# A two-block float32 network on one core: joint high and low products in the feed-forwards, squares added on GpSimd, and a first input in halves

## The reference, cut to what matters

```
x = x + 0.5 * swiglu(rms_norm(x, g), w_gate, w_up, w_down)      # four times, 1024 -> 2816 -> 1024
swiglu(h) = (silu(h @ w_gate) * (h @ w_up)) @ w_down
```

## Time and profile before

| | before |
|---|---|
| median of three runs | 2832.76 us |
| the profiled execution | 2852.74 us, its span 2851.3 us |
| TensorE busy | 2691.2 us (94%) |
| VectorE busy | 2021.0 us (71%) |
| ScalarE busy | 1560.1 us (55%) |
| GpSimd busy | 181.0 us (6%) |
| mean granted TensorE clock | 0.964 |

### The profile page before, as it was taken

How to read it: one execution, slowest core, us unless ns; L and a number is a source line. 1 busy time by engine, 2 the same in 40 slices (tenths; PEclk the granted TensorE clock), 3 DMA queues, 4 the chain that set the end, 5 groups by cost and what they waited for, 6 DMA issues and landing times.

```text
span 2851.3 us, 46825 instructions
## 1 busy us (share of the span) xinstructions
PE 2691.2 (94%) x19546; PEld 2453.9 (86%) x19546; DVE 2021.0 (71%) x2781; ACT 1560.1 (55%) x2162; POOL 181.0 (6%) x207
## 2 busy tenths in 40 slices
PE   7998899999898899999899996999999999999998
PEld 7997799999887888998899996788888888888887
DVE  5656755665565455658655675988989898988996
ACT  4445454444431224443544534786777777776785
POOL 1000000000002216001320010000000000000000
PEclk9999999999999769999999998999999999999999
DMA  6442234444333004453345431988989898988993
GB/s 231 178 178 104 104 134 178 179 177 178 138 121 117 3 3 178 179 187 134 122 178 179 157 134 65 376 342 313 355 336 354 332 355 342 355 334 313 357 371 119
DMA packets 84326, 605.09 MB, mean 212 GB/s; under 512 B 9368, under 2 KB 9496, under 8 KB 11472
## 3 DMA queue, kind: packets, MB, share of 16 engines
q1 hardware_dynamic: 81872, 594.05, 55.2%
q10 hardware_dynamic: 1888, 4.85, 0.5%
q0 software_dynamic: 352, 3.15, 0.3%
HBM read 600.96 MB, written 1.05 MB: 211 GB/s over the span
## 4 chain that ended last, share of the span: by engine, by line
PE 84%; DVE 11%; ACT 3%; issue 1%; DMA 1%; ACTq 0%; DVEq 0%
PE bank L396 82%; DVE weights_lo L386 2%; DVE arena L1884 2%; PE bank L2346 1%; ACT weights_hi L378 1%; DVE source_lo_scratch L1319 0%; DVE rstd L447 0%; DVE arena L503 0%; DMA raw_weights<-in_ffn_w_gate 0%; PE bank L807 0%; DMA x_T<-in_x 0%; DVE arena L1907 0%; PE bank L1488 0%; DVE arena L986 0%; DVE normed_T L454 0%
## 5 line engine op out<-in xcount | busy, mean ns | idle before, releaser
L386 DVE TENSOR_TENSOR weights_lo<-raw_weights,weights_hi 128x1024 fp32r<-128x1024 f32 x820 | 996.4, 1231 | 431.1 <-ACT weights_hi L378 424.7
L378 ACT CAST weights_hi<-raw_weights 128x1024 fp32r<-128x1024 f32 x820 | 853.1, 1050 | 472.1 <-PE bank L396 431.0
L396 PE MATMUL bank<-source_hi,weights_hi 128*128 128x256 f32 x2400 | 692.7, 289 | 56.6 <-DVE weights_lo L386 23.7
L396 PE MATMUL bank<-source_lo,weights_hi 128*128 128x256 f32 x2400 | 686.6, 286 | 0.0
L396 PE MATMUL bank<-source_hi,weights_lo 128*128 128x256 f32 x2400 | 686.3, 286 | 0.0
L396 PEld LDWEIGHTS bank<-source_hi,weights_hi 128*128 128x128 f32 x2400 | 468.4, 195 | 61.6 <-issue 36.4
L396 PEld LDWEIGHTS bank<-source_lo,weights_hi 128*128 128x128 f32 x2400 | 468.5, 195 | 1.0 <-issue 0.7
L396 PEld LDWEIGHTS bank<-source_hi,weights_lo 128*128 128x128 f32 x2400 | 468.2, 195 | 0.0
L396 PE MATMUL bank<-weights_hi,source_hi 128*128 128x512 f32 (+1 forms) x960 | 380.3, 396 | 0.0
L396 PE MATMUL bank<-weights_lo,source_hi 128*128 128x512 f32 (+1 forms) x960 | 368.6, 384 | 0.0
L396 PE MATMUL bank<-weights_hi,source_lo 128*128 128x512 f32 (+1 forms) x960 | 367.6, 383 | 0.0
(11 more groups left out here) (350 smaller groups left out, 3353.3 us busy)
## 6 DMA issues: line engine op xcount, KB each, us to landing
raw_weights<-in_exp_in SPq DMA_DIRECT2D x134, 1024.0 KB, 4.9
arena<-in_exp_in SPq DMA_DIRECT2D x90, 1024.0 KB, 4.9
raw_weights<-in_exp_w SPq DMA_DIRECT2D x67, 1024.0 KB, 5.0
arena<-in_exp_w SPq DMA_DIRECT2D x45, 1024.0 KB, 5.1
raw_weights<-in_ffn_w_gate SPq DMA_DIRECT2D x44, 1024.0 KB, 4.8
raw_weights<-in_ffn_w_up SPq DMA_DIRECT2D x44, 1024.0 KB, 4.9
raw_weights<-in_ffn_w_down SPq DMA_DIRECT2D x44, 1024.0 KB, 4.8
raw_weights<-in_dense_w SPq DMA_DIRECT2D x33, 1024.0 KB, 4.8
```

Source lines behind the costliest of these rows:

```text
L378: k.act.copy(k.weights(j)[0], raw_half(k, j)).then_inc(k.w_hi_ready, 1)
L386: k.dve.tensor_tensor(lo, raw_half(k, j), hi.bitcast(F32), ALU.subtract).then_inc(k.w_ready, 1)
L396: return k.pe.matmul(dst, lhsT, rhs, start=start, stop=stop, skip_group_check=shared)
```

## The change

1. In the five feed-forwards, gate and up take a joint product: the two source parts lie in one tile, and the high weights are multiplied with both in one matmul of 512 columns. Its high half goes to columns 0 to 255 of a bank and its low half to columns 256 to 511. The low weights by the high source are added into the first 256. So gate and up of a hidden block need one bank each: banks 0 to 3 for unit 0 and 4 to 7 for all later units. ScalarE copies the low half out of the bank, VectorE adds the high half to it (`low`, `total`), and only then come the root and the silu. The silu of the gate now stands ahead of the last weight split of up. Waits move with it: a later unit's gate waits for the sum of the gate before, and up for that of the up before; the first down also waits until unit 0's banks are empty.
2. The squares of a half feed-forward are added on GpSimd in three steps (4, 2 and 1 blocks), and TensorE takes one matmul against ones.
3. At the start x comes in two halves with a semaphore each, the constants are asked for without a wait, the first weight unit comes in two halves, and the first weight half is split after two source blocks, the second and third behind all of them, ahead of the squares. A tiny copy on ScalarE comes before any input is there.
4. `source_from_norm_vector` scales the blocks itself and makes the low part of block i-2 behind the scaling of block i.

The core of the diff:

```diff
+def mm_both(k, bank, w, at, kt):
+    here = slice(kt * T, (kt + 1) * T)
+    mm(k, bank[:, :].rearrange("p (w t) -> p w t", w=2), w[0][:, at], k.source_both[:, :, here], kt == 0, False, True)
+    return mm(k, bank[:, 0:T], w[1][:, at], k.source[0][:, here], False, kt == KT - 1, True)
+
+def unit_banks(k, i):
+    return [[k.bank[(4 if i else 0) + 2 * b + part] for part in range(2)] for b in range(2)]
...
-            squares_tensor(k, f, 7, KT)
+            k.pe.wait_ge(*k.square_sum.at((f, 1)))
+            mm(k, k.bank[7][:, 0:T], k.con("ones"), blk(k.sq, 0), True, True).then_inc(*k.norm_sums.step((f, "square")))
...
# ffn_scalar, per unit
+        split_both(split_hi, k, gate_name, first + i)
+        split_hi(k, up_name, first + i, 0)
+        k.act.wait_ge(*k.taken(gate_name, first + i))
+        for b in range(2):
+            low(i, b, k.act_buf, 0)
+        if not first_late:
+            silus(i)
+        split_hi(k, up_name, first + i, 1)
+        for b in range(2):
+            k.act.wait_ge(*(tr.products.at((f, i)) if b == 0 else k.taken(up_name, first + i)))
+            low(i, b, k.xn, 1)
+        if first_late:
+            root_scalar(k, f, 7, D, "eps_rms")
+            silus(i)
...
# ffn_vector, per unit
+        split_both(split_lo, k, gate_name, first + i)
+        split_lo(k, up_name, first + i, 0)
+        for b in range(2):
+            total(i, b, k.act_buf, 0, "gate_sum")
+        if late and i > 0:
+            for b in range(2):
+                rooted(i, b, k.act_buf, "gate_sum", "gate")
+        split_lo(k, up_name, first + i, 1)
+        for b in range(2):
+            total(i, b, k.xn, 1, "bank")
...
# half_ffn_scalar for the first feed-forward
+        elif i == 0:
+            k.act.wait_ge(k.params_landed, 16)
+            k.act.wait_ge(k.x_landed[0], 16)
+        elif i == 2:
+            split_hi(k, "ffn_w_gate", 0, 0, 1)
+        elif i == KT // 2:
+            k.act.wait_ge(k.x_landed[1], 16)
...
+    if which == 0:
+        for most in (2, 3):
+            split_hi(k, "ffn_w_gate", 0, 0, most)
...
+def half_ffn_gpsimd(k, which):
+    f = f"half{which}"
+    n = KT // 2
+    k.pool.wait_ge(*k.norm_roots.at((f, "square", KT - 1)))
+    while n > 0:
+        k.pool.tensor_tensor(k.sq[:, 0:n * T], k.sq[:, 0:n * T], k.sq[:, n * T:2 * n * T], ALU.add)\
+            .then_inc(*k.square_sum.step((f, n)))
+        k.pool.wait_ge(*k.square_sum.at((f, n)))
+        n //= 2
...
# source_from_norm_vector
+    for i in range(KT + 2):
+        if i < KT:
+            k.dve.scalar_tensor_tensor(blk(z, i), blk(z, i), k.col(gain, layer * KT + i), k.rstd[:, :], ALU.mult,
+                                       ALU.mult).then_inc(*k.normed.step((f, "scaled", i)))
+        if i >= 2:
+            k.dve.wait_ge(*k.src_hi.at((fill, i - 2)))
+            k.dve.scalar_tensor_tensor(low(i - 2), blk(z, i - 2), k.col(bias, layer * KT + i - 2), ...
```

More of the change, by code:

```diff
@@ L356, in raw_half, with ahead @@
     return k.raw_slots[k.slot[n]][:, part * HALF:(part + 1) * HALF]
-def ahead(k, name, i, part, done):
+def ahead(k, name, i, part, done, most=HALVES):
     n = k.unit[name, i]
@@ L369, in ahead, with split_hi @@
         done += 1
-def split_hi(k, name, i, part=None):
-    for j in ahead(k, name, i, part, k.hi_done):
-        if k.halves[j][1] == 0:
+def split_hi(k, name, i, part=None, most=HALVES):
+    for j in ahead(k, name, i, part, k.hi_done, most):
+        if j == 0:
+            k.act.wait_ge(k.first_landed, 16)
+        elif j == 1 or k.halves[j][1] == 0:
             k.act.wait_ge(*k.landed(k.halves[j][0]))
@@ L379, in split_hi, with split_lo @@
         k.hi_done = j + 1
-def split_lo(k, name, i, part=None):
-    for j in ahead(k, name, i, part, k.lo_done):
+def split_lo(k, name, i, part=None, most=HALVES):
+    for j in ahead(k, name, i, part, k.lo_done, most):
         hi, lo = k.weights(j)
@@ L576, in down_tensor @@
         k.pe.wait_ge(*tr.hidden.at((f, i, b, "lo")))
+        if i == 0 and b == 0:
+            k.pe.wait_ge(*tr.hidden.at((f, 0, 1, "bank")))
         for c in range(KT):
@@ L596, in ffn_scalar @@
             piece = blk(k.act_buf, j)
-            if late:
-                k.act.wait_ge(*tr.hidden.at((f, i, b, "gate")))
-                k.act.activation(piece, piece, ACT.Silu).then_inc(*tr.gates.step((f, i, b, "silu")))
-            else:
-                k.act.wait_ge(*(tr.products.at((f, i)) if b == 0 else k.taken(up_name, first + i)))
-                if i >= 2:
-                    k.act.wait_ge(*tr.hidden.at((f, i - 2, b, "lo")))
-                k.act.activation(piece, k.bank[4 + j][:, 0:T], ACT.Silu).then_inc(*tr.gates.step((f, i, b, "silu")))
@@ L605, in ffn_scalar @@
-            k.act.wait_ge(*tr.hidden.at((f, i, b, product)))
-            if i >= 2:
-                k.act.wait_ge(*k.taken(down_name, first + i - 2))
-            k.act.copy(blk(k.hidden[0], j), piece).then_inc(*tr.gates.step((f, i, b, "hi")))
-        if i > 0:
-            split_both(split_hi, k, down_name, first + i - 1)
-    split_both(split_hi, k, down_name, first + n - 1)
-def ffn_vector(k, f, tr, names, first, n, late=False, scale=None):
-    gate_name, up_name, down_name = names
-    for i in range(n):
-        for name in (gate_name, up_name):
-            split_both(split_lo, k, name, first + i)
-        if late and i == 0:
-            root_vector(k, f)
+            k.dve.wait_ge(*tr.gates.at((f, i, b, "silu")))
```

144 lines of the change are left out of this document (86 added, 58 removed).

## The result

| | before | after |
|---|---|---|
| median of 20 runs each, us | 2833.16 (2830.63 to 2852.03) | 2809.78 (2799.03 to 2836.09) |
| profiled execution, us | 2852.74 | 2827.23 (span 2825.8) |

The ratio after to before is 0.9915, with a 95% interval of 0.9895 to 0.9934: 23.4 us faster between the medians (the interval reaches from 19 to 30 us). Between the two profiled executions it is 25.5 us. I had forecast 2790 from a sum of 42.8.

The account below looks back on a forecast made before the run. TensorE was taken as the bound, with 84% of the span. Terms 23.3 + 12.0 + 7.7 - 1.5 + 2.3 - 1.0 = 42.8 us, subtracted from the median of 2832.8, gave 2790 us; range 2776 to 2812.

Parts of the forecast that it names:

- rival A: Gate and up products: the wide product saves next to nothing, 19 to 23.3 us lost, time 2810; chance 0.12.
- Triples: Gate and up blocks: one 512- and one 256-column product take 0.346 us against 0.360; 1710 x 13.6 ns = 23.3 us gained.
- Squares: Four half feed-forwards: seven products against ones fewer in each, 28 x 0.43 = 12.0 us gained if GpSimd's sums are in time.
- Start: Kernel start: first product at 11.3 us instead of 18.86; gain 7.7 us (5 to 9.5).
- GpSimd's lock: Attention tables' additions on GpSimd hold VectorE: TensorE's wait grows from 4.0 to about 5.5 us, taken as -1.5.
- Steady units: Later feed-forward units: added copies and additions on ScalarE and VectorE stay hidden with 2.4 us of slack; costed at nothing.
- the ring: ScalarE's order: up copies wait for TensorE's last up product, the next weight casts stand behind them and the silus; slack 2.4 us.
- rival C: Steady units: ScalarE's strict order exceeds the slack and each of 51 units pays; at 4 us over, 2872 us; chance 0.04.
- The unit-0 term: First unit of four half feed-forwards: TensorE may wait up to 1 us for a weight half; 0.25 each, 1.0 lost.
- Norms: Low parts made between scalings let TensorE start after 1.85 us instead of 3.80 at the dense norm; 2.3 us gained over three norms.

Follow-up runs that it names:

- the repeat: The changed kernel run again with no edit: median 2824.43 us of 10 runs, ratio 0.9951 to the kernel before.
- the bench: A small kernel without the network: trains of 24 pairs from ready memory, each behind something else; 0.3535 us a pair, 0.3465 right behind a float32 product.

## Why the prediction was right, and where its sum was not

Faster was right, and the time is inside the range, near its slow end, where rival A stood. That it lies inside owes something to luck: ten more runs of the same kernel had a median of 2824.43, outside the range. Their median clock was 0.964 against 0.9705, and the prediction had no term for the clock. The sum of 42.8 is 17 too high against the 25.5 between the two profiles, in which the recurrent stage happened to be equal (306.4 and 306.5). Two fifths of the forecast gain did not come.

- **Triples.** "1710 x 13.6 ns = 23.3 us" is the term that failed most. Measured 6.7 ns a triple by the trace, 6.1 by taking the joint product out and 6.6 by the dense stage with the old norm on both sides (4.3 there with the new norm): about 11 us in all. I had added the paces of two trains of one width each; mixed, they mostly cost 7 ns more. Rival A's result came about (half the gain gone, 12 us instead of its 20) by a mechanism that it named only as "no such mix of widths in this trace": its two pieces cost nothing. The Trainium skill's 2.5 ns for the fixed part of a product (TensorE: Matmul & The Clock Gate, the section on the back-to-back issue gap) is not borne out either: trains of 256 and 512 columns still show 13 ns each.
- **Squares.** 12.0 us counted; TensorE's train is 3.0 us shorter, as said. About 9 are left in the stages; in the first one the sums hold VectorE. They were in time everywhere.
- **Start.** 7.7 counted, 6.9 by the traces (TensorE is past the squares at 36.42 before and at 26.54 after, and 3.0 of the 9.9 are the squares), 7.9 in the repeat (25.56), 5.8 to 6.7 by undoing it. The step that was off: a first half of x at 8.0; it landed at 9.17. The term had the parameters as the only bound from below and left out the constants, which are now asked for at once; whether they held x up was not tried.
- **GpSimd's lock.** -1.5 counted, -1.25 in the profile (4.03 to 5.28); in the versions that leave it as it is the waits were 4.2 (the repeat, 0.86 and 3.38), 4.7, 4.9 and 4.9. Right, on the dear side.
- **Steady units.** Costed at nothing, and no wait for weights stands in them outside GpSimd's additions: the ring of rival C has slack. The unit-0 term, 0.25 in each of four, is there: in the second feed-forward the product at 391.09 comes 0.58 us behind that of the pair before instead of 0.35, and in the first one the wait is 0.55 to 0.82 in four profiles. The second feed-forward still gained 5.3, as 24 of its pairs ran at the fast pace.
- **Norms.** +2.3 counted. At the dense one the wait fell by 1.98 (my "1.9"), of which about 1.2 stayed. At the two second norms "the next split waits behind it and is needed 11 us on" was wrong: it was needed at 1581.8, when its remainder ended at 1583.8. That cost 3.1 and 1.7 us. The term is near -3.6.

The corrected terms: 11.5 + 9 to 12 + 6.3 - 1.25 - 3.6 = 22 to 25. Against them stand 25.5 between the profiles, of which about 1.6 is the clock in the third feed-forward.

The subtraction from the runs' median was unsafe. I took the 20 us between before's profile and its median for noise to be kept apart. They lie on the line of time against clock (0.964 and 0.973), and in the changed kernel's two profiles such a difference is that of the recurrent stage; its runs have their own share of it.

A version that keeps the joint product, the sums and the start, and writes x late, is the better one: ratio 0.9865 (0.9829 to 0.9900) against the kernel before, and 4.3 us under the changed kernel at equal clock, though by four runs only. Holding back the tables' additions gives 3 more at equal clock (2796.2), though its median of 9 runs, five of them at a clock of 0.967 or less, does not show it.

## What to carry to other kernels

Take the pace of a mixed train from a mixed train: two paces measured apart did not add up here (0.3535 against 0.347). When an engine's queue is put in another order, find what stands behind the moved work at each of its uses, not at the one you looked at: the same edit won 1.2 us at one norm and lost 4.8 at two. Where runs spread by more than the effect, plot time against granted clock first, and compare stages cut at common waits.

## What the runs showed of the hardware

- A 512-column and a 256-column product in turn take 0.3535 us or 0.347. In the bench the fast pace stood only right behind a float32 product and was gone with one 256-column product between; in the network whole units had it without one (0.3471 from 591.12 on). Grouped by four a pair takes 0.351. What chooses the pace is open.
- An operand read as two pieces costs what one piece costs (0.3535 both; 0.227 both for trains of it).
- The recurrent stage, 64-wide products, took 282.5 to 311.8 us in profiles of the same code, at clocks of 0.94 to 0.82, with the other engines busy for the same time. Float32 fill between them brought 354.8 at 0.76.
- Two transfers for x instead of one brought its first half in no earlier (9.17 us against 9.16 for the whole; 8.98 in the repeat). By 9.17 both kernels had moved 2.4 MB, and the whole first weight unit was in. In the changed kernel the constants and the second half of x were under way as well. Which of them held up the first half was not tried.
